# A decoder layer with 32 experts: the router ahead of the LayerNorm for the last tile, and another unit in the ninth buffer

## The reference

```
h = LayerNorm(ALPHA * x + mix) * ln1_g + ln1_b
logits = h @ w_router + b_router            # 32 experts
top 4 of the logits, softmax over them
for every chosen expert e: hh = h @ w_gu[e] + b_gu[e]   # 1024 x 2048
    act = (clip(up) + 1) * gate * sigmoid(1.702 gate)
    f  += weight * (act @ w_down[e] + b_down[e])        # 1024 x 1024
y = LayerNorm(ALPHA * h + f) * ln2_g + ln2_b
```

## Time and profile before

| | us |
|---|---|
| median of 3 runs | 1268.34 |
| profiled execution, its own time | 1269.73 |
| its span | 1268.0 |
| PE busy | 1162.3 (92%) |
| DVE busy | 467.2 (37%) |
| ACT busy | 248.4 (20%) |
| POOL busy | 27.5 (2%) |
| bytes moved | 454.50 MB, mean 358 GB/s |

### The profile page before, as it was taken

The page is one execution under the profiler, slowest core; times in us unless marked ns, Lnnn a source line. Parts: engine busy times, 40 slices in busy tenths (PEclk is TensorE's granted clock), DMA queues, the critical chain, the costliest instruction groups (busy, mean ns, idle before and its releaser), DMA issues.

```text
span 1268.0 us, 15570 instructions
## 1 busy us (share of the span) xinstructions
PE 1162.3 (92%) x6265; PEld 640.4 (50%) x6265; DVE 467.2 (37%) x796; ACT 248.4 (20%) x407; POOL 27.5 (2%) x44
## 2 busy tenths in 40 slices
PE   6999999999999999998898899989898988898884
PEld 6999999998543433433343234334333423343331
DVE  4575666665533232322222231223222222322135
ACT  4544344420211111111111111111111101110112
POOL 0000100100000000000000000000000000000001
PEclk9999999999899999999999999999999999999997
DMA  9526444692499999999999999999999999999993
GB/s 380 204 101 241 137 170 158 230 365 83 167 428 423 428 427 427 426 428 427 428 428 428 427 428 428 428 427 428 429 427 427 428 429 427 427 428 428 427 424 132
DMA packets 37945, 454.50 MB, mean 358 GB/s; under 512 B 4461, under 2 KB 4589, under 8 KB 9096
## 3 DMA queue, kind: packets, MB, share of 16 engines
q1 hardware_dynamic: 33744, 439.62, 83.0%
q0 software_dynamic: 4160, 14.29, 3.3%
HBM read 447.70 MB, written 6.31 MB: 358 GB/s over the span
## 4 chain that ended last, share of the span: by engine, by line
DMA 51%; PE 44%; DVE 3%; ACT 1%; issue 1%; SPq 0%; DVEq 0%; ACTq 0%
DMA ring<-in_w_gu 31%; DMA ring<-in_w_down 19%; PE bank L1009 13%; PE bank L706 12%; PE bank L1037 6%; PE bank L774 3%; PE bank L749 2%; PE bank L1061 1%; PE bank L982 1%; PE bank L833 1%; PE bank L820 1%; DMA ring<-in_w_mix 1%; PE bank L761 1%; DVE arena L1626 1%; PE bank L823 1%
## 5 line engine op out<-in xcount | busy, mean ns | idle before, releaser
L1009 PE MATMUL bank<-ring,arena 128*64 128x512 f32 x1504 | 339.8, 599 | 44.0 <-DMA ring<-in_w_gu 44.0
L1009 PEld LDWEIGHTS bank<-ring,arena 128*64 128x64 f32 x1504 | 103.7, 137 | 258.7 <-issue 182.8
L1037 PE MATMUL bank<-ring,arena 128*64 128x512 f32 x784 | 178.7, 598 | 18.0 <-DMA ring<-in_w_down 17.7
L706 PE MATMUL bank<-arena_r,ring_r 128*128 128x320 f32 x848 | 182.3, 316 | 0.0
L1865 DVE SCALAR_TENSOR_TENSOR arena_r<-bank,arena,arena_r 64x512 fp32r<-64x512 f32 x62 | 46.4, 749 | 289.5 <-ACT arena_r L1408 289.0
L706 PEld LDWEIGHTS bank<-arena_r,ring_r 128*128 128x128 f32 x848 | 138.7, 188 | 0.6 <-issue 0.4
L1828 DVE COPY arena<-bank 128x512 f32<-128x512 f32 x32 | 22.1, 692 | 290.6 <-PE bank L1009 290.6
L1009 PE MATMUL bank<-arena 128*64 128x512 f32 x528 | 119.8, 596 | 7.7 <-DMA arena<-in_w_gu 7.4
L1037 PEld LDWEIGHTS bank<-ring,arena 128*64 128x64 f32 x784 | 54.1, 136 | 121.9 <-issue 99.3
L1396 ACT ACTIVATE arena<-bank 128x512 f32<-128x512 f32 x32 | 19.1, 598 | 423.4 <-PE bank L1009 423.4
L1499 DVE TENSOR_TENSOR ring_r<-ring,ring_r 128x1024 fp32r<-128x1024 f32 x56 | 67.8, 1224 | 56.5 <-ACT ring_r L1225 56.3
(11 more groups left out here) (258 smaller groups left out, 957.8 us busy)
## 6 DMA issues: line engine op xcount, KB each, us to landing
ring<-in_w_gu SPq DMA_DIRECT2D x94, 2048.0 KB, 35.0
ring<-in_w_down SPq DMA_DIRECT2D x48, 2048.0 KB, 35.1
arena<-in_w_gu SPq DMA_DIRECT2D x33, 2048.0 KB, 35.2
ring<-in_w_mix SPq DMA_DIRECT2D x32, 1024.0 KB, 5.2
arena<-in_w_down SPq DMA_DIRECT2D x15, 2048.0 KB, 35.1
arena<-in_state_gla POOLq DMA_DIRECT2D x4, 1024.0 KB, 6.8
out<-arena POOLq DMA_DIRECT2D x4, 1024.0 KB, 5.6
alone<-in_w_gu SPq DMA_DIRECT2D x1, 2048.0 KB, 9.3
```

Source lines behind the costliest of these rows:

```text
L706: last = mm(o[:, 0:NT], w[a][:, c, f0:f0 + 128], rhs[b][:, c, :], start=c == 0 and a + b == 0, stop=c == chunks - 1 and a == 1)
L1009: last = mm(ex[i][side * CAP:(side + 1) * CAP, :], xgt[:, 2 * j + c, block * CAP:(block + 1) * CAP], w[:, c, i * D + side * 512:i * D + (s ...
L1037: last = mm(out[side * CAP:(side + 1) * CAP, :], actt[:, 4 * j + c, :], w[:, c, side * 512:(side + 1) * 512], start=j == 0 and c == 0, sto ...
```

## The change

Three edits, all with effect before or at the start of the experts.

1. **The router ahead of the LayerNorm, tile 1.** The gain of ln1 is multiplied into the router's weights, and the sums over channels of weight times gain and weight times bias are made once (`wr_gain`, `wr_bias`, `wr_sums`; DVE, behind the copy of `pb`). A product with ones, `fold`, adds them over the partitions; DVE reads it behind the splits of gb(5). PE transposes the sum `xr` itself in four blocks (`turn_block`), as each output product is added, and the router works on those (`router_block`). DVE corrects the logits by mean and deviation.
2. **LayerNorm of tile 1 on three engines, gather in f32.** DVE makes columns 0 to 511 (it then counts `rank` and makes `oh1` in float32, and the f32r one-hot behind it), ACT whitens columns 512 to 1023 and POOL applies gain and bias. The gather of tile 1 uses `hrow` itself with a float32 one-hot (`last_gather`) instead of two parts; the parts are made later. The two halves of the first gather stand on either side of the ranks. The twelve products of `keep_clock` become four. The token count moves behind the first unit of the first expert.
3. **The ninth buffer.** `alone` holds unit 8 (the first down unit of expert 0) instead of unit 0. Refill n for n up to 16 waits for unit n-9, later ones for n-8 as before.

```diff
-            + [("pb",), ("up",), ("us",)] + [("gb", i) for i in range(6)] + [("grp", i) for i in range(4)]
+            + [("pb",), ("up",), ("us",), ("fold",)] + [("gb", i) for i in range(6)] + [("grp", i) for i in range(4)]
-            + [("lg", 0), ("out", 2, 1), ("rk", 0), ("out", 3, 1), ("ht", 1, 0), ("ht", 1, 1), ("lg", 1)]
+            + [("lg", 0), ("xb", 0), ("out", 2, 1), ("rk", 0), ("xb", 1), ("out", 3, 1), ("xb", 2), ("lg", 1), ("xb", 3)]
-EARLY = 1
+LONE = 8
...
         def place(n):
-            return n - EARLY if n < EARLY else (n - EARLY) % SLOTS
+            return -1 if n == LONE else (n - (n > LONE)) % SLOTS
...
-                was_up, e, j = unit_at(n - SLOTS)
+                was_up, e, j = unit_at(n - SLOTS - (n - SLOTS <= LONE))
```

POOL, behind the loads of ln1:

```diff
+            pool.wait_ge(white1, 1)
+            nc.gpsimd.tensor_tensor(upper, upper, ln1[0][:, 512:], ALU.mult).then_inc(gain1, 1)
+            pool.wait_ge(gain1, 1)
+            nc.gpsimd.tensor_tensor(upper, upper, ln1[1][:, 512:], ALU.add).then_inc(h1_ready, 1)
             pool.wait_ge(*full(("lg", 1)))
```

PE, between `us` and `gb`, and its new functions and order behind the output projection:

```diff
+            pe.wait_ge(fold_ready, 1)
+            o = claim(("fold",))
+            mm(o[:, 0:2 * NE], cst("ones"), wr_sums.rearrange("p a e -> p (a e)"), start=True, stop=True)\
+                .then_inc(full(("fold",))[0], 1)
             for i in range(6):
                 weights_times("gb", i, xt)
...
+            def turn_block(j):
+                pe.wait_ge(freed(("out", j, 1)), NO[("out", j, 1)] // 8 + 1)
+                o = claim(("xb", j))
+                for c in range(2):
+                    f0 = j * 256 + c * 128
+                    last = nc.tensor.transpose(o[:, c * 128:(c + 1) * 128], xr[:, 1, f0:f0 + 128], ident)
+                last.then_inc(full(("xb", j))[0], 1)
+            def router_block(j):
+                pe.wait_ge(xb_ready, j + 1)
+                for c in range(2 * j, 2 * j + 2):
+                    last = mm(bank(("lg", 1))[:, 0:NE], ot[:, c, 128:256], wr_gain[:, c, :], start=c == 0, stop=c == KC - 1)
+            def last_gather(half):
+                for c in range(4 * half, 4 * half + 4):
+                    last = mm(ex[6 + half][:, (c % 4) * 128:(c % 4 + 1) * 128], hrow[:, 1, c * 128:(c + 1) * 128], oh1,
+                              start=False, stop=True, skip_group_check=True)
+                last.then_inc(gathered, 1)
...
             ranks(2, 2)
             router(0, 4)
+            turn_block(0)
             tokens_times("out", 2, 1, ga)
             ranks(0, 3)
+            turn_block(1)
             tokens_times("out", 3, 1, ga)
+            turn_block(2)
+            claim(("lg", 1))
+            router_block(0)
+            router_block(1)
+            turn_block(3)
+            router_block(2)
+            router_block(3).then_inc(full(("lg", 1))[0], 1)
             released(6)
...
-            for half in range(2):
-                first_gather(ORDER[:2], half, True)
+            first_gather(ORDER[:2], 0)
+            ranks(1, 4)
+            released(7)
+            first_gather(ORDER[:2], 1)
             spare = claim(("gwt",))
             keep_clock(2)
-            turn_h(1, 5)
-            keep_clock(2)
-            router(1, 6)
-            keep_clock(6)
-            ranks(1, 4)
...
```

PE, ahead of the experts:

```diff
-            pe.wait_ge(onehot_ready, 1)
-            pe.wait_ge(parts_ready, 3)
-            for half in range(2):
-                first_gather(ORDER[2:], half, False).then_inc(gathered, 1)
+            pe.wait_ge(oh1_ready, 1)
+            pe.wait_ge(h_ready, 5)
+            last_gather(0)
+            pe.wait_ge(h1_ready, 1)
+            last_gather(1)
+            keep_clock(2)
-            expert_up(units(True, 0), 0, gathers=1)
+            expert_up(units(True, 0), 0, gathers=1, between=[count_tokens], after=(0,))
```

ACT, for tile 1:

```diff
+            for j in range(4):
+                if j == 3:
+                    act.wait_ge(var_ready, 3)
+                    A(rstd, mv[:, 1:2], ACT.Sqrt, bias=eps_ln).then_inc(std_ready, 1)
+                act.wait_ge(*full(("xb", j)))
+                A(ot[:, 2 * j:2 * j + 2, 128:256], bank(("xb", j))[:, 0:256].rearrange("p (c n) -> p c n", n=128), ACT.Copy)\
+                    .then_inc(xb_ready, 1)
+                act.wait_ge(xb_ready, j + 1)
+                act.sem_inc(freed(("xb", j)), 1)
+            act.wait_ge(shift1_ready, 1)
+            A(hrow[:, 1, 512:], xr[:, 1, 512:], ACT.Identity, scale=rstd, bias=shift1).then_inc(white1, 1)
```

DVE, behind the copy of `pb` and the wait for `us`:

```diff
+            V.tensor_tensor(wr_gain, wrt, cols[:, 26:34].unsqueeze(2).broadcast_to([128, KC, NE]), ALU.mult)
+            link(V.tensor_tensor(wr_bias, wrt, cols[:, 34:42].unsqueeze(2).broadcast_to([128, KC, NE]), ALU.mult))
+            V.tensor_reduce(wr_sums[:, 0, :], wr_gain.rearrange("p c e -> p e c"), mybir.AxisListType.X, ALU.add)
+            V.tensor_reduce(wr_sums[:, 1, :], wr_bias.rearrange("p c e -> p e c"), mybir.AxisListType.X, ALU.add)\
+                .then_inc(fold_ready, 1)
```

DVE, behind the splits after gb(5), ahead of the `grp` products:

```diff
+            dve.wait_ge(*full(("fold",)))
+            V.tensor_scalar(wr_rows[:, 0, :], bank(("fold",))[:, 0:NE], -1.0, None, ALU.mult)
+            V.tensor_tensor(wr_rows[:, 1, :], bank(("fold",))[:, NE:2 * NE], brt, ALU.add).then_inc(fold_done, 1)
+            dve.wait_ge(fold_done, 1)
+            dve.sem_inc(freed(("fold",)), 1)
```

DVE, tile 1, behind its statistics:

```diff
+            link(V.scalar_tensor_tensor(lower_half, xr[:, 1, 0:512], mv[:, 0:1], ln1[0][:, 0:512], ALU.subtract, ALU.mult))
+            dve.wait_ge(std_ready, 3)
+            link(V.reciprocal(rstd, rstd))
+            V.scalar_tensor_tensor(shift1, mv[:, 0:1], -1.0, rstd, ALU.mult, ALU.mult).then_inc(shift1_ready, 1)
             route(2, 1)
+            V.scalar_tensor_tensor(lower_half, lower_half, rstd, ln1[1][:, 0:512], ALU.mult, ALU.add).then_inc(h_ready, 1)
...
```

DVE, in `route`, for tile 1:

```diff
+            link(V.scalar_tensor_tensor(lg[:, 1, :], wr_rows[:, 0, :], mv[:, 0:1], bank(("lg", 1))[:, 0:NE], ALU.mult, ALU.add))
+            link(V.scalar_tensor_tensor(lg[:, 1, :], lg[:, 1, :], rstd, wr_rows[:, 1, :], ALU.mult, ALU.add))
```

More of the change, by code:

```diff
@@ L144 @@
 WRT = GA2 + 640
+OH1 = WRT + 256
+FOLD = BB + 1088
 SP = 17408
@@ L421, in build @@
         onehot_ready = sem("onehot_ready")
+        fold_ready = sem("fold_ready")
+        fold_done = sem("fold_done")
+        xb_ready = sem("xb_ready")
+        shift1_ready = sem("shift1_ready")
+        white1 = sem("white1")
+        gain1 = sem("gain1")
+        h1_ready = sem("h1_ready")
+        oh1_ready = sem("oh1_ready")
         parts_step = sem("parts_step")
@@ L589, in _ @@
                     sp.wait_ge(*full(FREE_AFTER[i]))
-                load_unit(*unit_at(i + EARLY), i)
-            first = UNIT_SEQ[(True, 3, 0)]
-            for n in range(SLOTS + EARLY, first):
+                load_unit(*unit_at(i), i)
+            first = LONE + SLOTS + 1
+            for n in range(SLOTS + 1, first):
                 next_unit(n)
@@ L909, in released, with first_gather @@
                 pe.wait_ge(bank_free[n], LAST_USE[n])
-            def first_gather(tiles, half, first):
+            def first_gather(tiles, half):
                 for c in range(4 * half, 4 * half + 4):
@@ L915, in first_gather @@
                         for a in range(2):
[L916 to L919, removed]
+                            mm(ex[6 + half][:, (c % 4) * 128:(c % 4 + 1) * 128], h_parts[a][t][:, c * 128:(c + 1) * 128],
+                               onehot[:, 0, t, :], start=t == tiles[0] and a == 0 and c % 4 == 0,
+                               stop=False, skip_group_check=True)
+            def last_gather(half):
[3 more added lines that the diff above has]
+                last.then_inc(gathered, 1)
             def keep_clock(n):
@@ L946, in _, with count_tokens @@
             pe.wait_ge(parts_ready, 2)
-            for half in range(2):
-                first_gather(ORDER[:2], half, True)
+            first_gather(ORDER[:2], 0)
+            ranks(1, 4)
+            released(7)
+            first_gather(ORDER[:2], 1)
             spare = claim(("gwt",))
             keep_clock(2)
-            turn_h(1, 5)
-            keep_clock(2)
-            router(1, 6)
-            keep_clock(6)
-            ranks(1, 4)
[L956 to L960, removed]
+            def count_tokens():
+                o = claim(("cnt",))
+                for t, (t0, n) in enumerate(TILES):
+                    last = mm(o[0:1, 0:NE], cst("ones", p=n, n=1), msk[0:n, t, :], start=t == 0, stop=t == 2)
+                last.then_inc(full(("cnt",))[0], 1)
             def gather_pair(pair):
@@ L1360, in turned_h @@
                         .then_inc(ht_ready, 1)
-            for i, t in enumerate(ORDER):
+            for i, t in enumerate(ORDER[:2]):
                 n = TILES[t][1]
@@ L1806, in _ @@
                         first_onehot(0).then_inc(onehot_early, 1)
[L1807 to L1811 removed]
+                if t == 0:
+                    link(centred(xr[:, t, :], hrow[:, t, :], 128, t + 2, ln1[0], rstd))
```

(22 more changed lines are left out.)

45 lines of the change are left out of this document (32 added, 13 removed).

## The result

The changed kernel takes 1280.31 us (median of 4 runs, 1278.26 to 1281.86); the kernel before took 1267.12 in the same comparison. The ratio is 1.0104, 95% interval 1.0082 to 1.0125. A second comparison on another occasion gave 1279.91 against 1266.45 (15 runs of before), 1.0102 (1.0087 to 1.0117). So it is slower by 13 us. The profiled executions differ by less, 1280.22 against 1269.73: the one profiled of the kernel before lies 2.6 us above that kernel's median of 1267.12.

A forecast was written before the change was run, and what follows sets the result against it. PE was taken as the limit before about 340 us, the DMA weight stream after; +13.1 us ahead of T' and -5.3 behind it made +7.8, 1276.1 us as median, own range 1272 to 1279, 8 in 10 1268 to 1281.

The forecast's parts named there:

- The rival with falls of the clock at full price: Clock falls in both stalls and on the router path at full price: +11.6 us, 1279.9; chance 0.2.
- the two waits and their releasers: PE idle about 3.5 us before gb, released by DVE's reduction, and 3.9 us before the second grp product.
- the pause of the stream ahead of unit 18: DMA share falls for some 3 us just ahead of weight unit 18, whose slot unit 10 must free.
- The fold's stall: PE waits for fold_ready with all gb products queued behind; gb begins at 234.3 instead of 230.52: +3.75 us.
- The fold's bank: grp(1) gets fold's bank, which DVE frees only at 256.0 while PE wants it at 252.2: +3.85 us.
- The clock in the stalls: PE's clock likely falls to half in each of the two stalls: 2.5 us each, bounds 0 and 3.4.
- Two turn_blocks: Two block transposes on PE before the last output product, hidden by nothing: +0.5 us.
- T': The new end of the last output projection, from which the forecast counts; in the kernel before, T was 316.24 us.
- The router path: From output projection to first expert: T'+11.0 instead of T+14.6, with 1.4 us taken as lost to the clock.
- POOL beside the routing: GpSimd's two LayerNorm operations beside DVE's routing slow it, the comparison by the skill's rule: 0.6 us, bounds 0 and 1.35.
- The slot edit: Earlier first refill only makes the queue run dry 3.1 us before unit 18, which waits for unit 10; gain 0.7 us.
- The base: Sum built on the profiled execution's 1269.73 us, with the median of the runs shown taken as 1.4 lower.

The follow-up runs named there:

- e2_read_early: Changed kernel with DVE reading the fold and freeing its bank behind the first window group, not behind the splits after gb(5): 1274.77 us, ratio 1.0061.
- e0_after_again: The changed kernel run once more with no edit, as base for other runs: 1279.91 us, ratio 1.0102 against the kernel before.
- e5_filled: Changed kernel with 22 unused products ahead of the wait for fold_ready and 24 ahead of the claim of grp(1): 1276.02 us, ratio 1.007.
- e7_keepers: Changed kernel with the fold behind gb(7) and six more clock keepers on the router path: 1264.47 us, ratio 0.9987 against the kernel before.
- e4_slots_alone: The kernel before with only the third edit, unit 8 in the ninth buffer: 1265.66 us, ratio 0.9994.
- e8_both: Changed kernel with the fold behind gb(7), POOL's LayerNorm operations behind the mask, three more clock keepers: 1264.68 us, ratio 0.998 against the kernel before.

## Why the prediction was right, and where it was off

The direction, the mechanism and the place were right, and 1280.3 lies in the range for 8 in 10. It lies outside the forecast's own range of 1272 to 1279: the likeliest time was 4 us too low. The rival with falls of the clock at full price (1279.9) came closest, but in part by luck. It put 6.8 us on the clock in the stalls, where some 3 to 4 were measured, and 3.4 on the router path, where it was 4.6. Of the signs named, the two waits and their releasers, the fallen clock behind them, the end of the output projection (328.16) and the pause of the stream ahead of unit 18 (213 GB/s from 392 to 395 us) came as said. The first expert did not: 10 to 12 us behind the output projection were named, and it came after 15.8.

- **The fold's stall.** Forecast 3.75 to the start of gb. In the profile 4.3: 3.64 idle, and the fold's own product 0.69 at half clock where 0.2 was taken. The releaser is the reduction, as named.
- **The fold's bank.** Forecast 3.85; 3.83 idle, released by DVE's increment of that bank. Numbering the products by hand gave it; e2_read_early shows it on its own.
- **The clock in the stalls.** Forecast 2.5 each. In the profile 1.2 in gb, and 1.7 in grp (5.52 less 3.83). In e0_after_again, the same kernel, 2.6 in gb and 0.7 in grp. e5_filled gives 3.9 for both. So 5.0 together was somewhat high, and how the clock's loss divides on the two stalls changes from one execution to the next.
- **Two turn_blocks.** Forecast 0.5; 0.25 each in the chain. The sum ahead of T' was 13.1 and came out as 11.9, of which 0.5 were there before the fold and are no part of the change.
- **The router path.** Here the prediction was off in size. It forecast the first expert at T'+11.0 and allowed 1.4 for the clock. It came at T'+15.8. Of these 4.8 us the clock is 4.6: with the clock held in e7_keepers, and all other steps the same, the first expert comes at T'+11.2. So the working was right but for the clock term, which was 1.4 and should have been over 4. Its bound of 3.4 was too low as well: the clock was down for 10.3 us and not for 6.8. The gain behind T' was forecast at 5.3 and was 1.7 (68.4 - 66.7).
- **POOL beside the routing.** Forecast 0.6, measured 0.9, on another operation than the one named: the cast and not the comparison. GpSimd's half was in time, as forecast.
- **The slot edit.** Forecast 0.7 and a pause of the stream ahead of unit 18. The pause is there in e4_slots_alone and e8_both; the gain is about 1 us by the profiles.
- **The base.** The profiled execution of before was 2.6 us above its median as later runs give it (1267.12), and not 1.4. Forecast was +7.8. The two profiled executions differ by 10.5 and the medians by 13.2. So 2.7 of the missing 5.4 us are the terms above, and 2.7 are that the sum was built on an execution of the kernel before that was not a typical one.

What stays open: how long the clock stays down. The profiled executions gave 3 to 7 us behind a stall and 7 to 10 us on the router path. The kernel before has a fall of its own, and its length varies too: 6.8 us in the earlier trace rows, but some 3.3 us in e4_slots_alone (a mean of 0.59 over 4.0 us), which has the same work there:

```profile
325.00:329.80 4.80, 4.51 (x32) 3.45 (x32) 3.42 (x22) 0.30 (x2) 1.98 (x4) 1.00 0.26 82
329.90:333.90 4.00, 4.00 (x16) 1.98 (x17) 3.79 (x21) 1.94 (x3) 0.00 (x0) 0.59 0.02 4
334.00:338.00 4.00, 4.00 (x22) 1.28 (x20) 3.51 (x15) 0.00 (x0) 0.00 (x0) 1.00 0.40 80
```

So part of the spread of the kernel before may be this. It would also explain why e7's profile is 5.4 us shorter in span than the one of before (1262.6 against 1268.0) while the medians differ by 1.7. The mean granted clock of every run fits it. Of the 23 runs of the kernel before beside e8, the 18 at 1265.4 to 1267.2 us have 0.993 to 0.996, one at 1268.4 has 0.994, and the four at 1269.7 to 1270.0 have 0.991 or 0.992. The 12 runs of e8 fall in two halves: 1262.4 to 1263.7 us with 0.995 or 0.996, and 1265.6 to 1266.3 with 0.992 to 0.994. Where the clock fell in a run without a profile stays unknown: only one execution of the kernel before has a profile here.

Two comparisons are missing. No run adds clock keepers to the kernel before, whose clock falls in the same place, so how much of the final 1.7 to 2.5 us is the new order and how much the keepers is not known. And the first two edits were never run apart.

## What to carry to other kernels

When a step is taken ahead, price what it issues where it is put: one small product, placed behind a wait for an engine that is a step late and in a rotation of banks that is eight deep, cost 11 us, and what it was to make possible came to 1.7 us by the medians once it was placed well and the clock held, with the keepers' part in that not separated. Look up who gets the new item's buffer next, and what the engine that frees it does first. A stall on TensorE is dearer than its length, by half here; where the waiting can't be avoided, products that nobody reads keep the clock, and where it can, move the product.

## What the runs showed of the hardware

The clock can fall under full work. In e8's execution it went down near 37 us, in the mixer, where PE was busy without a gap:

```profile
36.00:38.00 2.00, 2.00 (x9) 1.48 (x8) 1.93 (x3) 0.00 (x0) 0.00 (x1) 0.74 1.01 379
38.00:40.00 2.00, 2.00 (x9) 2.00 (x8) 1.86 (x4) 0.00 (x0) 0.00 (x0) 0.50 0.98 358
```

It was back at 1.00 near 40.4 us. The 72 records of the mixer's product there take 12.31 us, and 10.77 in the kernel before, so this fall cost 1.5 us. No other profiled execution has one in the mixer away from the two stalls. In that of the kernel before the clock was down from 1155.3 to 1158.7 us, among the experts: PE was busy throughout that stretch, but only for 2.4 of the 5 us ahead of it; there PE waits for weights, and what the fall cost is not known.

A DVE operation with a single input of eight elements per partition can be held by GpSimd as well as one with two inputs: the cast above waited 0.9 us, while the search for the index just before it (one input and the values loaded) was not held.
